# A two-block kernel: experts ordered by token count, tokens gathered once

## What is computed

```
expert_id = g_sel[..., None] * EXPERTS_PER_GROUP + top_i          # top_k of 2 in the best group
combine = jnp.sum(jax.nn.one_hot(expert_id, N_EXPERTS) * w_top[..., None], axis=-2)
y = jnp.zeros_like(h)
for e in range(N_EXPERTS):
    a = jax.nn.silu(h @ lp['w_gate'][e]) * (h @ lp['w_up'][e])    # 1024 -> 512
    y = y + combine[..., e, None] * (a @ lp['w_down'][e])         # 512 -> 1024
```

## Time and profile before

| | |
|---|---|
| median of 3 runs | 1132.5 us |
| the profiled execution, time | 1132.93 us |
| the profiled execution, span | 1131.0 us |
| TensorE busy | 1025.3 us (91% of the span), granted clock 0.938 |
| VectorE busy | 665.2 us (59%) |
| ScalarE busy | 401.0 us (35%) |
| HBM read | 263.19 MB, of which experts' weights 108 x 1 MB |

### The profile page before, as it was taken

How to read it: one execution, slowest core, us unless ns; L and a number is a source line. 1 busy time by engine, 2 the same in 40 slices (tenths; PEclk the granted TensorE clock), 3 DMA queues, 4 the chain that set the end, 5 groups by cost and what they waited for, 6 DMA issues and landing times.

```text
span 1131.0 us, 14937 instructions
## 1 busy us (share of the span) xinstructions
PE 1025.3 (91%) x6028; PEld 803.6 (71%) x6028; DVE 665.2 (59%) x1318; ACT 401.0 (35%) x622; POOL 72.4 (6%) x110
## 2 busy tenths in 40 slices
PE   4997989999999997889999998999777899998895
PEld 4876779999999786789999997857654344433342
DVE  5899579898764899478889556352645401010102
ACT  6452533434533253434343336336322111111111
POOL 1202000000000002000000000003510000000000
PEclk8997989999996997989999999999967899999998
DMA  9515075674534415168777553101057999999994
GB/s 373 216 75 223 1 296 222 227 297 186 188 143 183 158 67 223 53 283 323 293 312 287 187 217 140 75 18 57 1 225 314 380 422 421 421 420 421 421 421 185
DMA packets 31879, 264.99 MB, mean 234 GB/s; under 512 B 4048, under 2 KB 4176, under 8 KB 5840
## 3 DMA queue, kind: packets, MB, share of 16 engines
q1 hardware_dynamic: 31824, 264.25, 58.4%
HBM read 263.19 MB, written 1.05 MB: 234 GB/s over the span
## 4 chain that ended last, share of the span: by engine, by line
PE 70%; DVE 13%; DMA 10%; issue 3%; ACT 2%; POOL 1%; SPq 0%; DVEq 0%; POOLq 0%
PE bank L659 16%; PE bank L661 16%; PE bank L660 16%; DMA blocks_w<-in_experts 6%; PE bank L1175 6%; PE bank L650 5%; PE bank L1192 4%; DVE scratch L1696 3%; DMA m<-in_experts 2%; DVE w_l L1651 2%; PE bank L1140 1%; PE bank L674 1%; DMA m<-in_w_in 1%; PE bank L1001 1%; DVE scratch L1764 1%
## 5 line engine op out<-in xcount | busy, mean ns | idle before, releaser
L661 PE MATMUL bank<-h_h,fw_l 128*128 128x256 f32 x800 | 225.4, 282 | 0.0
L659 PE MATMUL bank<-h_h,fw_h 128*128 128x256 f32 x704 | 199.0, 283 | 6.5 <-issue 6.5
L660 PE MATMUL bank<-h_l,fw_h 128*128 128x256 f32 x704 | 198.3, 282 | 0.0
L1871 DVE TENSOR_TENSOR fw_l<-blocks_w,fw_h 128x1024 fp32r<-128x1024 f32 x132 | 156.2, 1219 | 3.4 <-ACT fw_h L1373 3.2
L661 PEld LDWEIGHTS bank<-h_h,fw_l 128*128 128x128 f32 x800 | 152.2, 190 | 0.0
L659 PEld LDWEIGHTS bank<-h_h,fw_h 128*128 128x128 f32 x704 | 134.0, 190 | 9.0 <-issue 7.3
L660 PEld LDWEIGHTS bank<-h_l,fw_h 128*128 128x128 f32 x704 | 134.1, 190 | 1.9
L1373 ACT ACTIVATE fw_h<-blocks_w 128x1024 fp32r<-128x1024 f32 x132 | 129.7, 1051 | 4.3 <-DMA blocks_w<-in_ffn 4.3
L1175 PE MATMUL bank<-m,scratch 128*64 128x512 f32 x368 | 99.6, 595 | 9.2 <-DMA m<-in_experts 6.6
L1399 ACT ACTIVATE acts<-bank 128x256 f32<-128x256 f32 x44 | 17.0, 386 | 213.6 <-PE bank L661 213.6
L1914 DVE SCALAR_TENSOR_TENSOR m<-m,scratch 128x512 f32<-128x512 f32 x128 | 90.1, 745 | 0.0
(11 more groups left out here) (352 smaller groups left out, 2029.4 us busy)
## 6 DMA issues: line engine op xcount, KB each, us to landing
m<-in_experts SPq DMA_DIRECT2D x64, 1024.0 KB, 18.7
blocks_w<-in_ffn SPq DMA_DIRECT2D x22, 2048.0 KB, 7.6
blocks_w<-in_experts SPq DMA_DIRECT2D x44, 1024.0 KB, 22.3
m<-in_w_ada SPq DMA_DIRECT2D x24, 1024.0 KB, 8.3
m<-in_w_in SPq DMA_DIRECT2D x11, 2048.0 KB, 9.3
blocks_w<-in_ffn SPq DMA_DIRECT2D x22, 1024.0 KB, 4.9
m<-in_w_out SPq DMA_DIRECT2D x6, 2048.0 KB, 7.5
blocks_w<-in_w_in SPq DMA_DIRECT2D x2, 2048.0 KB, 19.6
```

The costliest lines, as they stand in the source:

```text
L659: pe.matmul(out_, xh, wh, start=first and i == 0, stop=False, skip_group_check=True)
L660: pe.matmul(out_, xh, wl, start=False, stop=False, skip_group_check=True)
L661: ins = pe.matmul(out_, xl, wh, start=False, stop=last and i == n - 1, skip_group_check=True)
L1871: dve.tensor_tensor(fw_l[:, slot, at], blocks_w[:, slot, at], f32(fw_h[:, 1 - slot, at]), ALU.subtract)\
```

## The change

Experts 0 to 3 stay in two pair passes, (0,1) and (2,3). The other 12 are put in order of token count by a table that VectorE computes from the counts, and are addressed by chunk number, 4 being the fullest. The passes are (0,1), (2,3), (4), (6,7), (5), (8,9), (10,11), (12,13), (14,15), and then four overflow pairs inside the `If`. A pass of one expert gives it all 128 slots. There is no longer a pass of overflow chunks outside the `If`; the `If` is entered when any chunk is left over (experts 0 to 3 or the third fullest and later with more than 64 tokens, or more than 128 in the two fullest). The weights of passes from the third on are loaded with expert numbers from the table. The ring keeps 7 pieces; a one-expert pass has 3 of them and not 6.

The tokens of the first two passes are gathered as before. For all others `choice_all` holds 512 slots, one for each assignment, ordered by expert; eight gathers of 4 matmuls, 512 slots wide, run in passes 0 and 1 and leave all tokens in `xg_all`. For each later pass ScalarE reads the expert's first slot from the table into a register and copies 64 or 128 slots into `xg` (`next_slots`), and TensorE waits for that copy (`xg_ready`).

The diff, cut to its core:

```diff
 NE, EPG, NG = 16, 4, 4
 DE = 512
 CAP = 64
-MAIN = NE // 2 + 1
-EXTRA = 3
-NPASS = MAIN + EXTRA
-NCHUNK = 2 * NPASS
-OVER = NCHUNK - NE
-ROUNDS = NPASS // 2
+FIXED = 4
+SORTED = NE - FIXED
+OVER = 8
+NCHUNK = NE + OVER
+PASSES = [(0, 1), (2, 3), (4,), (6, 7), (5,)] + [(c, c + 1) for c in range(8, NCHUNK, 2)]
+NPASS = len(PASSES)
+MAIN = NPASS - OVER // 2
 RING = 7
-PICKS, TURNS = 4, 3
+PICKS = TURNS = 4
+PAIRS = 2 * T
+USERS = [(p, kind) for p in range(NPASS) for kind in range(3) for _ in PASSES[p]]
+PIECES = {(p, kind): USERS.index((p, kind)) for p in range(NPASS) for kind in range(3)}
+T_OFF, T_OVER = NE + OVER - FIXED, 2 * (NE + OVER - FIXED)
 GRID_W, POS_BASE, ROPE_THETA = 64, 10000.0, 10000.0
@@ -97,9 +102,7 @@
             self.count[bank] += times
-GATHERS = [[(p // 2 + 1, 2 * (p % 2) + c) for c in range(2)] for p in range(MAIN - 1)]
-GATHERS += [[]] + [[(ROUNDS - 1, c) for c in range(4)]] + [[] for _ in range(MAIN + 1, NPASS)]
-CHOSEN = [p % 2 == 1 and p < NPASS - 2 for p in range(NPASS)]
...
-            b.add(7, f"eg{r}{c}")
+        if p == MAIN:
+            b.add(7, f"es{p}")
+        for k in GATHERED.get(p, ()):
+            b.add(7, f"eg{k}")
         b.add(6, f"eh{p}")
-        if CHOSEN[p]:
-            b.add(6, f"es{p + 1}")
-            b.add(7, f"es{p + 2}")
+        if 0 < p < NPASS - 1 and p + 1 != MAIN:
+            b.add(7, f"es{p + 1}")
...
+            def load_pass(p, experts):
+                for kind in range(3):
+                    for h in range(2):
+                        for e, expert in enumerate(experts):
+                            n = PIECES[p, kind] + e
+                            src = half_piece(expert, kind, h)
+                            if n >= RING:
+                                used_p, used = USERS[n - RING]
+                                if h == 0:
+                                    sp.wait_ge(first_half[used], used_p + 1)
+                                else:
+                                    sec.ready(sp, (f"eG{used_p}", f"eU{used_p}", f"eD{used_p}1")[used])
+                            sp.dma_start(ring[n % RING][:, h * 2048:(h + 1) * 2048], src).then_inc(piece_in[n % RING][h], 16)
...
+            for p in range(FIXED // 2, MAIN):
+                load_pass(p, chosen_experts(p))
+            with sp.If(sp.value_load(table_i[0:1, T_OVER:T_OVER + 1], min_val=0, max_val=OVER) > 0):
                 for p in range(MAIN, NPASS):
...
                     pieces_arrived(p, kind, h)
                     for k in range(4 * h, 4 * h + 4):
-                        for e in range(2):
-                            ins = pe.matmul(to(name)[e * CAP:(e + 1) * CAP, :],
-                                            xg[:, p // 2 % 2, k, p % 2 * P + e * CAP:p % 2 * P + (e + 1) * CAP],
-                                            ring[(6 * p + 2 * kind + e) % RING][:, k * 512:(k + 1) * 512],
+                        for e, rows in parts(p):
+                            ins = pe.matmul(to(name)[rows, :], xg[:, p % 2, k, rows],
+                                            ring[(PIECES[p, kind] + e) % RING][:, k * 512:(k + 1) * 512],
...
+            def gathered(p, half):
+                ks = GATHERED.get(p, ())
+                if len(ks):
+                    pe.wait_ge(sorted_ready, 1)
+                for k in ks[2 * half:2 * half + 2]:
+                    gather(f"eg{k}", k, 512, lambda t: choice_all[:, t, :])
             def expert_pass(p):
                 if p == 0:
                     for c in range(4):
                         sec.arrived(pe, f"first{c}")
-                elif p % 2 == 0:
-                    sec.arrived(pe, f"eg{p // 2}3")
+                elif p >= FIXED // 2:
+                    pe.wait_ge(xg_ready, sum(len(q) for q in PASSES[FIXED // 2:p + 1]))
                 for kind, name in enumerate((f"eG{p}", f"eU{p}")):
                     sec.room(pe, name)
-                    pair_product(p, kind, name)
-                pieces = GATHERS[p]
-                if pieces:
-                    pe.wait_ge(choice_ready, pieces[0][0] + 1)
...
-                        transposed_choice(f"es{n}", n)
+                gathered(p, 1)
+                if 0 < p < NPASS - 1 and p + 1 != MAIN:
+                    pe.wait_ge(choice_ready, p + 1)
+                    transposed_choice(f"es{p + 1}", p + 1)
                 sec.arrived(pe, f"eh{p}")
-                pair_down(p)
+                expert_down(p)
...
+            def gathered_all(p, half):
+                for k in GATHERED.get(p, ())[2 * half:2 * half + 2]:
+                    sec.ready(act, f"eg{k}")
+                    sec.moved(act.activation(xg_all[:, k, 0:PAIRS], to(f"eg{k}")[:, :], ACT.Identity, scale=modc[:, 3, k, 0:1],
+                                             bias=modc[:, 2, k, 0:1]), f"eg{k}")
+            def next_slots(p):
+                w = P // len(PASSES[p])
+                for e, c in enumerate(PASSES[p]):
+                    at = T_OFF + c - FIXED
+                    first = act.value_load(table_i[0:1, at:at + 1], min_val=0, max_val=PAIRS)
+                    act.activation(xg[:, p % 2, :, e * w:(e + 1) * w], xg_all[:, :, bass.ds(first, w)], ACT.Copy)\
+                        .then_inc(xg_ready, 1)
...
-                    for n in (p + 1, p + 2):
-                        act.wait_ge(slot_ready, n + 1)
-                        choices(f"es{n}", n)
+                gathered_all(p, 1)
+                if p == 1:
+                    act.wait_ge(table_ready, 1)
+                    act.wait_ge(pad_ready, 1)
+                    for k in range(KD):
+                        sec.arrived(act, f"eg{k}")
+                if 0 < p < NPASS - 1 and p + 1 != MAIN:
+                    next_slots(p + 1)
+                    act.wait_ge(slot_ready, p + 2)
+                    choices(f"es{p + 1}", p + 1)
                 act.wait_ge(slot_ready, p + 1)
...
+            slots(0, place_e)
+            slots(1, place_e).then_inc(choice_ready, 1)
+            fixed = slice(0, FIXED)
+            S.then(dve.tensor_copy(comb[:, :, fixed], comb_e[:, :, fixed]))
+            split_weights(fixed)
             weights(0)
             weights(1).then_inc(first_weights, 1)
-            count = to("rank")[:, 2 * NE:3 * NE]
-            S.then(dve.tensor_scalar(over_x, count, CAP + 0.5, None, ALU.is_gt))
...
+            ins.then_inc(sorted_ready, 1)
             for n in range(2):
                 slot_weights(f"first_sT{n}", n)
-            choose(1)
+            cand = slice(FIXED, NE)
+            steps = const[:, K_SLOT:K_SLOT + NE]
+            by_size = masked.rearrange("p t d e -> p (t d e)")[:, 0:SORTED * SORTED].rearrange("p (d e) -> p d e", d=SORTED)
+            S.then(dve.scalar_tensor_tensor(key, count[:, cand], float(NE), const[:, K_RANK + FIXED:K_RANK + NE], ALU.mult, ALU.add))
+            S.then(dve.tensor_tensor(by_size, key.unsqueeze(1).to_broadcast([P, SORTED, SORTED]),
+                                     key.unsqueeze(2).to_broadcast([P, SORTED, SORTED]), ALU.is_ge))
...
+            dve.tensor_copy(table_i[:, :], table).then_inc(table_ready, 1)
+            expert_hidden(0)
             for t in range(NT):
-                S.then(dve.scalar_tensor_tensor(place_f[:, t, :], over_f, float(CAP), place[:, t, 0:NE], ALU.mult, ALU.add))
...
-            with dve.If(dve.value_load(table_i[0:1, OVER:OVER + 1], min_val=0, max_val=OVER) > 2):
+            with dve.If(dve.value_load(table_i[0:1, T_OVER:T_OVER + 1], min_val=0, max_val=OVER) > 0):
+                slot_weights(f"es{MAIN}", MAIN)
                 for p in range(MAIN, NPASS):
                     expert_pass(p)
             gated_add("ye", 10, 1, out_ready)
```

More of the change, by code:

```diff
@@ L2120, in _ @@
                 S.did(dve.tensor_copy(pick_w[:, i, 4:4 + P], ident))
+            for i in range(PAIRS // P):
+                S.did(dve.tensor_scalar(iota[:, i * P:(i + 1) * P], const[:, K_SLOT:K_SLOT + P], float(P * i), None, ALU.add))
             dve.wait_ge(router_in, 32)
@@ new lines, in _, with picked @@
+            S.then(dve.tensor_tensor(over_f, over_f, over_1, ALU.subtract))
+            S.then(dve.scalar_tensor_tensor(start_o, over_f, -float(CAP), start, ALU.mult, ALU.add))
+            def picked(dst, rows, values):
+                n = rows.shape[1]
+                part = masked[:, 0, 0:n, :]
+                S.then(dve.tensor_tensor(part, rows, values.unsqueeze(1).to_broadcast([P, n, NE]), ALU.mult))
+                S.then(dve.tensor_reduce(dst, part, AX.X, ALU.add))
+            main_w, over_s = which[:, 0:SORTED, :], slice(SORTED, SORTED + OVER)
@@ new lines, in _ @@
+            for rows, at in ((main_w, slice(0, SORTED)), (over_w, over_s)):
+                picked(table[:, at], rows, const[:, K_RANK:K_RANK + NE])
+            S.then(dve.tensor_scalar(table[:, 0:T_OFF], table[:, 0:T_OFF], 1.0, -1.0, ALU.max, ALU.mult))
+            S.did(dve.tensor_scalar(table[:, 0:T_OFF], table[:, 0:T_OFF], float(NE), None, ALU.add))
```

(3 more changed lines are left out.)

248 lines of the change are left out of this document (137 added, 111 removed).

## The result

| | before | after |
|---|---|---|
| time, median of the runs (us) | 1132.41 (1131.41 to 1132.77, 4 runs) | 1101.93 (1100.09 to 1104.97, 4 runs) |
| profiled execution: time, span (us) | 1132.93, 1131.0 | 1100.09, 1098.3 |
| ratio of the times | | 0.9733 (0.9713 to 0.9753) |

The change makes the kernel 30.5 us faster, 2.7%. I had forecast 1109 and a range of 1103 to 1118; 1101.9 lies under its low end.

A forecast was written before the change was run, and what follows sets the result against it. TensorE was to bound the kernel until pass 5 and DMA from there. Last product at 1093.7 us plus a 13.1 us tail gave a span of 1106.8 and, with the time around the span, 1109 us, range 1103 to 1118.

The forecast's parts named there:

- Ahead of pass 0 I cost nothing: Before the expert stage: the added iota instructions and `choice_all` (about 4 us) fall into waits, so no time is added.
- Twelve halves at 2.495 us: Weights' queue: 96 halves of 1 MB instead of 108, worth 29.9 us if DMA were all.
- Only 24 of the 29.9 us are seen, as TensorE becomes the bound: Expert stage: TensorE bounds until pass 5, so the last product ends at 1093.7 instead of 1117.9, 24.2 us earlier.
- A late pass takes 23.8 us: Passes without gathers: 23.8 us of TensorE each, 3.0 less than an odd and 1.4 less than an even pass of before.
- Pass 0 27.1, pass 1 30.2 us: First two passes, which carry all gathers: 27.1 and 30.2 us of TensorE, with 0.9 us for waits on bank 7.
- The clock stays at 1.00 in pass 0: TensorE in pass 0: new stops of 0.9 us leave the granted clock at 1.00; the 27.1 us assume this.
- rival (d): Low clock in pass 0 again: 2 us more, 1111 us; chance 0.80 together with the main forecast.
- The idle 3.67 us go: TensorE in pass 0: idle time of 3.67 us goes, since the gathers last until 884.2 anyway.
- ScalarE's loads and copies hide in 5.5 us: ScalarE between the copy of hidden and y: 2.8 us added, within 5.5 us, leaving 2.6 to spare.
- Rival (a): Passes longer than counted, by ScalarE's loads and copies or switching between 64 and 128 columns: 1117 us; chance 0.11.
- Ring full, then DMA-bound: the last pass waits for weights, in all 2.4 us: Queue stands with a full ring, then bounds from pass 5; the last product ends 2.4 us behind TensorE's own count.
- Rival (b): DMA stays the bound throughout, as late passes are faster than thought and the ring is never full: 1100 us; chance 0.04.

The follow-up runs named there:

- e1: Kernel before with only its int32 table widened from 9 to 41 columns, so `scratch` starts 128 bytes higher: 1123.95 us, ratio 0.9918.
- e6: Changed kernel with every pass a pair, eight passes, further tokens of the two fullest experts left out: 1092.75 us, ratio 0.9657.
- e7: Changed kernel with its two one-expert passes at places 5 and 6 instead of 2 and 4: 1098.86 us, ratio 0.9693 to before.
- e8: Changed kernel with one-expert passes at places 5 and 6 and the gathers spread over several PSUM banks: 1095.96 us, ratio 0.968 to before.
- e5: Kernel before without its ninth pass and the extra passes behind the `If`, 96 halves: 1102.19 us, ratio 0.9733.
- e2: Changed kernel with its table widened by another 32 columns, so `scratch` starts at 128 bytes modulo 256 as before: 1111.36 us, ratio 0.9816.
- e4: Changed kernel with the `If` condition made true for every count, so the four spare passes run: 1220.97 us.
- e9: Kernel before with its integer table widened from 9 to 73 columns, moving `scratch` by 256 bytes: 1134.19 us, ratio 1.0003.
- e3: Kernel before with pass 0's hidden multiply taken ahead of the last two of eight overflow blocks on VectorE: 1131.6 us, ratio 0.9991.

## Why the prediction was wrong, step by step

- **The sentence that failed** is "Ahead of pass 0 I cost nothing". I had counted VectorE's few instructions there, and they were hidden, as I said; but I took it that unchanged code takes unchanged time. The wider table moved `fw_h` by 128 bytes, and two feed-forward stretches of 11 blocks each got 0.39 us a block faster: 8.6 us by the issue rows, 8.5 by e1. Pass 0 started 10.1 us early in the profiled execution, which was itself 1.8 us under the median; in the profiled executions of after, e1, e6, e7 and e8, which share the placement, it starts between 857.3 and 860.8, so 1.5 us beyond the 8.6 need no cause of their own. No part of the forecast had a place for it. The diff had it (a buffer's width), and I read that line for its meaning alone.
- **Twelve halves at 2.495 us**: right, 30.3 us for 29.9 (e5).
- **Only 24 of the 29.9 us are seen, as TensorE becomes the bound**: right in kind. Without the placement 21.1 us were seen (e2) where I had 23.7; some 1.5 of the 2.6 missing us are the slow clock in pass 1 of e2's profiled execution. e6 shows the rest of the 29.9 behind the one-expert passes.
- **A late pass takes 23.8 us**: 23.46 to 23.59, some 1.5 us too much over the six that don't wait; the last takes 27.5, 1.3 us more than I had. A one-expert product takes 13.97 us for gate and up and 7.08 for down, as worked out.
- **Pass 0 27.1, pass 1 30.2 us**: 28.3 and 30.7. The waits for bank 7 that I had at 0.9 us came at 0.87, but a pair of gathers takes 3.1 us in pass 0 and not 2.75, since four gather matmuls take 1.04 us, or 1.2 where something waits for their end, and not 0.93. And there is a third wait in pass 0, 0.52 us, which I didn't have: the second pair's first gather needs bank 7 while ScalarE is at its copy of 0.78 us. The two passes are 1.7 us longer than forecast, and six of the later ones 1.5 shorter, so these errors cancelled by luck:

```profile
873.28 0.50 PE L1154 MATMUL bank<-choice_all,xn_h 128*128 128x512 f32 x1 [0.87 <-ACT scratch L1585]
...
875.44 0.47 PE L1154 MATMUL bank<-choice_all,xn_h 128*128 128x512 f32 x1 [0.52 <-ACT scratch L1585]
```

```profile
906.01 0.78 ACT L1585 ACTIVATE scratch<-bank,scratch 128x512 f32<-128x512 f32 x1 [1.25 <-PE bank L1154]
```

- **The clock stays at 1.00 in pass 0**: right, 1.00 through stops of 0.87, 0.52 and 0.87 us, where the stop of 3.67 us before had been followed by 0.53. The down product takes 7.09 us again. But rival (d) was not wrong in kind. Pass 1 has stops of 0.87, 0.87 and 0.96 us, and behind them the clock fell in the profiled executions of e2 (0.57 for 4 us) and e4 (0.69 for 4 us), while in those of after, e6 and e7 the same stops left it at 1.00. So short stops can cost some 1.5 us, and that none of it is in after's profiled execution is luck. The 1.3 us that I took for the slow clock in pass 0 of before is no fixed price either: behind the same stop of 3.65 to 3.67 us the down product took 7.20 us (e5) to 8.47 us (e9). The Trainium skill ("TensorE: Matmul & The Clock Gate", section "What's actually happening") has the slow clock as the default and steady activity as what releases it. The rows agree as far as they go: the clock fell only behind stops, and was back at 1.00 once TensorE had been busy again (in e2 from 922 us on).
- **The idle 3.67 us go**: they went, but the credit was not theirs. e3 took them out of before and gained about 1 us, as the queue was the bound there.
- **ScalarE's loads and copies hide in 5.5 us**: right, there is still idle time of 4.16 us ahead of the first y:

```profile
932.57 1.28 ACT L1594 ACTIVATE scratch<-scratch 128x512 f32 x2
...
938.28 0.69 ACT L1624 ACTIVATE y<-bank,scratch 128x512 fp32r<-128x512 f32 x1 [4.16 <-PE bank L1211]
```

  Rival (a) fell with it.
- **Ring full, then DMA-bound: the last pass waits for weights, in all 2.4 us**: 3.0 us, and the end of the last product is 227.8 us behind the first (226.2).
- **Tail 13.1 us**: 1085.2 to 1098.3, 13.1.
- **Rival (b), 1100 us by the queue alone**: near the time that came, but for another reason. The queue was held up by the full ring in the middle, as its dips show, so (b)'s mechanism did not act. A number near the result does not show the cause that it was worked out from.

## What to carry to other kernels

A change that makes a small buffer wider moves all that is placed behind it. Before forecasting, list which buffers move against which, and try one kernel with the move alone; and before judging any change, compare the pace of the stretches that it does not touch. Where a ring feeds TensorE, freeing a slot earlier is worth at most the idle time of the queue, and time taken off TensorE is worth it only until the queue is late again.

## What the runs showed of the hardware that was not expected

- TensorE's pace in feed-forward matmuls, at full clock and without gaps, depends on how the buffers lie against each other: 16.91 us a block, 16.52 with `scratch` moved by 128 bytes, 16.82 by 64, 16.91 again by 256, 16.72 with `scratch` and `acts` moved together by 128, and 16.91 with everything moved by 128.
- Stops of 0.87 to 0.96 us on TensorE, close together, were followed by a granted clock of 0.57 or 0.69 in two profiled executions and left it at 1.00 in three others.
- The weights' queue moved 421 GB/s into a ring that starts at 128 within 256 bytes and 426 to 427 GB/s into one that starts at a multiple of 256.
- A scaled activation with an addend out of PSUM takes 0.78 us for 128x512, a plain one 0.60.
